# Moving part of a value-page weighting from TensorE to GpSimd and VectorE, with a later attention schedule and an earlier squaring of x

## The reference, cut to what matters

```
h = rms_norm(x, norm1_w);  z = h @ w_in          # conv, q, k, v, memory q and three gates
q, k = partial_rope(rms_norm(...))               # 8 heads, two halves of 64 each
s = einsum('bqhcd,bkhcd->bhcqk', q, k) * 64**-0.5
p = softmax(s);  a = p[:, :, 0] - lam * p[:, :, 1]
o = einsum('bhqk,bkhd->bqhd', a, v)              # prompt: own rows; samples: 16 pages + own row
o = rms_norm(o, subln_w) * 0.8
y_mem = mem_attn(qm, mem_k, mem_v) @ w_cross_out # 4 heads into 256 memory tokens
merged = g0 * y_conv + g1 * (y_diff or y_mem) + ...;  x = x + merged @ w_o
x = x + peer_ffn(rms_norm(x, norm2_w))           # top-16 of 16384 experts, 8 heads, gathered rows
```

## Time and profile before

| | us |
|---|---|
| median of 3 runs | 2854.64 |
| lowest, highest | 2852.84, 2857.38 |
| profiled execution, device time | 2857.79 |
| its span | 2855.9 |
| PE busy in the span | 2478.5 (87%) |
| DVE, POOL, ACT busy | 1390.6 (49%), 1038.9 (36%), 355.1 (12%) |

### The profile page before, as it was taken

The page is one execution under the profiler, slowest core; times in us unless marked ns, Lnnn a source line. Parts: engine busy times, 40 slices in busy tenths (PEclk is TensorE's granted clock), DMA queues, the critical chain, the costliest instruction groups (busy, mean ns, idle before and its releaser), DMA issues.

```text
span 2855.9 us, 28287 instructions
## 1 busy us (share of the span) xinstructions
PE 2478.5 (87%) x9241; PEld 1592.3 (56%) x9241; DVE 1390.6 (49%) x2168; ACT 355.1 (12%) x760; POOL 1038.9 (36%) x952
## 2 busy tenths in 40 slices
PE   6899999979999999999998687777899587777777
PEld 4777788868766668888776333232333133223333
DVE  2365566862112213000057687876555655556543
ACT  2111000012221111000120211101011011111010
POOL 1165566020122210000015556556445443555442
PEclk9999999989999999999999899999899889999999
DMA  5499999594598975443459999999999989999999
GB/s 156 153 335 319 316 337 335 192 332 153 195 339 322 330 275 180 155 138 119 146 200 355 401 421 417 417 417 411 422 422 416 413 360 422 418 421 417 421 422 376
DMA packets 305393, 913.67 MB, mean 320 GB/s; under 512 B 15634, under 2 KB 195946, under 8 KB 236652
## 3 DMA queue, kind: packets, MB, share of 16 engines
q0 software_dynamic: 122304, 723.48, 63.0%
q1 hardware_dynamic: 182980, 188.92, 20.3%
HBM read 905.80 MB, written 6.56 MB: 319 GB/s over the span
## 4 chain that ended last, share of the span: by engine, by line
PE 53%; DMA 25%; DVE 12%; issue 5%; POOL 4%; ACT 1%; DVEq 0%; POOLq 0%; ACTq 0%; SPq 0%
PE ps L573 20%; PE ps L651 12%; DMA sb_S<-in_peer_u_dram,sb_ring 10%; DMA sb_bregion<-in_peer_u_dram,sb_ring 6%; PE ps L663 6%; PE ps L878 4%; DMA sb_mkv<-in_peer_u_dram,sb_ring 3%; PE ps L641 3%; PE ps L751 2%; DVE sb_bregion L1765 2%; DMA sb_wring<-in_w_in_dram 2%; DVE sb_S L1765 2%; DMA sb_S<-in_peer_v_dram,sb_ring 1%; POOL sb_bregion L486 1%; POOL sb_wring L486 1%
## 5 line engine op out<-in xcount | busy, mean ns | idle before, releaser
L878 PE MATMUL ps<-sb_wring,sb_ring 128*128 128x512 f32 x992 | 462.7, 617 | 129.7 <-DMA sb_wring<-in_peer_v_dram,sb_ring 80.8
L573 PE MATMUL ps<-sb_hT,sb_wring 128*128 128x264 f32 x2304 | 533.4, 393 | 18.2 <-DMA sb_wring<-in_w_peer_q_dram 8.7
L573 PEld LDWEIGHTS ps<-sb_hT,sb_wring 128*128 128x128 f32 x2304 | 442.2, 193 | 101.5 <-issue 23.1
L878 PEld LDWEIGHTS ps<-sb_wring,sb_ring 128*128 128x128 f32 x992 | 189.0, 197 | 404.2 <-issue 270.4
L1765 DVE CUSTOM_DVE_ANT_0 sb_bregion<-sb_bregion,sb_rows 128x2048 f32<-128x2048 f32 x128 | 293.6, 2294 | 228.7 <-DMA sb_bregion<-in_peer_u_dram,sb_ring 221.6
L651 PE MATMUL ps<-sb_hT,sb_wring 128*128 128x264 f32 x1536 | 365.8, 389 | 9.2 <-issue 6.8
L651 PEld LDWEIGHTS ps<-sb_hT,sb_wring 128*128 128x128 f32 x1536 | 286.5, 190 | 74.8 <-issue 27.7
L486 POOL DMA_INDIRECT sb_bregion<-in_peer_u_dram,sb_ring x132 | 187.2, 1419 | 280.2 <-DVEq L1183 228.0
L878 PE MATMUL ps<-sb_hT,sb_ring 128*128 128x512 f32 x496 | 234.9, 623 | 46.2 <-DMA sb_hT<-in_peer_v_dram,sb_ring 35.0
L878 PE MATMUL ps<-sb_oreg,sb_ring 128*128 128x512 f32 x496 | 223.4, 597 | 39.8 <-DMA sb_oreg<-in_peer_v_dram,sb_ring 37.2
L1150 ACT ACTIVATE sb_ring<-sb_ident,sb_ring 128x128 f32<-128x128 f32 x248 | 99.6, 402 | 909.5 <-PE ps L878 702.1
(11 more groups left out here) (349 smaller groups left out, 2530.2 us busy)
## 6 DMA issues: line engine op xcount, KB each, us to landing
sb_wring<-in_w_in_dram SPq DMA_DIRECT2D x52, 2048.0 KB, 13.3
sb_ring<-in_cache_k_dram POOLq DMA_DIRECT2D x64, 512.0 KB, 6.5
sb_mkv<-in_cache_k_dram POOLq DMA_DIRECT2D x64, 512.0 KB, 6.8
sb_mkv<-in_cache_v_dram POOLq DMA_DIRECT2D x48, 512.0 KB, 6.9
sb_rows<-in_cache_v_dram POOLq DMA_DIRECT2D x47, 512.0 KB, 7.0
sb_wring<-in_w_mem_kv_dram SPq DMA_DIRECT2D x8, 2048.0 KB, 8.8
sb_wring<-in_w_o_dram SPq DMA_DIRECT2D x8, 2048.0 KB, 8.1
sb_wring<-in_w_peer_q_dram SPq DMA_DIRECT2D x8, 2048.0 KB, 13.7
```

Of the source, the lines that this page charges most:

```text
L573: last = mm(ps[:, (2 * r + c) % 4, 0:NT], wring[:, r, k, c * P:(c + 1) * P], rhs[:, k, :], start=(k == 0), stop=(k == KC - 1))
L878: last = mm(ps[:, 4 * t + q, :], diag[:, k % 4, :], e_slots[v % ER][:, q * 512:(q + 1) * 512], start=False, stop=q_stop, skip_group_check= ...
```

## The change

Three things, in one diff:

1. **Start.** DVE squares x first; the `lam` products come after the copies into `hT`, the column copies after the row factors. The rows of x are no longer multiplied by their factors: DVE multiplies the identity by them (three small tiles), and PE's 16 x 3 transposes become fp32 products with these diagonals.
2. **Units.** Every step of the sample softmax comes later by about a unit, and head `a` runs in units 2a+2 and 2a+3. `turn_maxima(0)` goes from (0, 15) to (1, 23). The branch product of unit 1 goes to bank 5, so that it need not wait for the merge of unit 0.
3. **Value pages.** PE weighs pages 0 to 7 of a sample, in 2 rounds: (odd unit, 18) and (even unit, 10). Pages 8, 9, 11, 13, 14 are multiplied in place by POOL, 10, 12, 15 by DVE, and DVE adds 9 to 15 into page 8, and that into `own_heads` behind `mask_sums`. Page 8 has two slots of its own, the other 15 pages share nine in a ring.

```diff
+        PE_PAGES, BY_POOL, BY_DVE = 8, (8, 9, 11, 13, 14), (10, 12, 15)
+        ORDER = (8, 9, 0, 1, 2, 3, 10, 11, 12, 4, 5, 6, 7, 13, 14, 15)
+            elif n == PE_PAGES:
+                slot = b % 2
+            else:
+                slot, ringed = 2 + ringed % 9, ringed + 1
+        def page_freed(page):
+            if n < PE_PAGES:
+                return "vpage_used", MEM_PAGES + PE_PAGES * b + n + 1
+            if n == PE_PAGES:
+                return "own_summed", b + 1
+            return "page_added", (PAGES - PE_PAGES - 1) * b + n - PE_PAGES
...
+            def weigh_page(b, n):
+                pool.wait_ge(v_landed[slot], 16 * (page_use[b, n] + 1))
+                st(nc.gpsimd.tensor_tensor(page, page, Ad[:, b, n, :].unsqueeze(2).broadcast_to([P, HEADS, DV]), ALU.mult))
+                pool.sem_inc(s["page_weighed"], 1)
-            for p in range(MEM_PAGES, VPAGES):
-                load_page(p)
+            BEHIND = 6
+            for i, (b, n) in enumerate(page_loads):
+                load_page(b, n)
+                if i >= BEHIND and page_loads[i - BEHIND][1] in BY_POOL:
+                    weigh_page(*page_loads[i - BEHIND])
...
-                transpose_rows(x_rows, k, k % 8, TILES).then_inc(s["xT_full"], 1)
+                for t, (first, n) in enumerate(TILES):
+                    last = mm(ps[:, k % 8, first:first + n], x_rows[0:n, t, k * P:(k + 1) * P], small[0:n, t, 0:n], start=True, stop=True)
+                last.then_inc(s["xT_full"], 1)
...
-                pe.wait_ge(s["y_taken"], q + 2)
+                pe.wait_ge(s["y_taken"], q + 2 if bank == 2 else 2)
...
-                pe.wait_ge(s["sums_masked"], m + 1)
+                    pe.wait_ge(s["own_summed"], m - MEM_ROUNDS + 1)
...
-                if (q, k) == (0, 15):
+                if (q, k) == (1, 23):
                     turn_maxima(0, nk)
-                a = (q - 1) // 2
+                a = (q - 2) // 2
-                if 11 <= q < 27 and k in (6, 18):
-                    value_round(MEM_ROUNDS + 2 * (q - 11) + k // 18)
+                if 11 <= q < 27 and (q % 2, k) in ((1, 18), (0, 10)):
+                    value_round(MEM_ROUNDS + q - 11)
...
-            for t in (0, 2):
-                st.run(TSC(x_rows[0:n, t, :], x_rows[0:n, t, :], stat[0:n, t:t + 1], None, ALU.mult))
+            for t, (_, n) in enumerate(TILES):
+                st.run(TSC(small[0:n, t, 0:n], ident[0:n, 0:n], stat[0:n, t:t + 1], None, ALU.mult))
...
+                b = (q - 11) // 2
                 if 13 <= q < 29 and q % 2:
+                    mask_sums(MEM_ROUNDS + b - 1)
+                    add_sums(b - 1)
+                if 11 <= q < 27 and q % 2:
+                    weigh_page(b, 10)
+                    add_page(b, 9)
+                    add_page(b, 10)
+                    weigh_page(b, 12)
+                    add_page(b, 11)
+                    add_page(b, 12)
+                if a < ATTN and q % 2 == 0:
                     maxima_of(a)
+                    if 11 <= q < 27:
+                        add_page(b, 13)
+                        weigh_page(b, 15)
                     normalise(a)
+                    add_page(b, 14)
+                    add_page(b, 15)
```

More of the change, by code:

```diff
@@ L645, in _, with gate_chunk @@
             own_scores()
-            def gate_chunk(b, r, c, q, operand, landed, between=None, ready=None):
+            def gate_chunk(b, r, c, q, operand, landed, between=None, ready=None, bank=2):
                 pe.wait_ge(s["gate_done"], q + 1)
@@ L662, in gate_chunk @@
                 for k in range(BC):
-                    last = mm(ps[:, 2, 0:NT], bwring[:, r, k, c * P:(c + 1) * P], operand[:, k, :], start=(k == 0), stop=(k == BC - 1))
+                    last = mm(ps[:, bank, 0:NT], bwring[:, r, k, c * P:(c + 1) * P], operand[:, k, :], start=(k == 0), stop=(k == BC - 1))
                     if k == BC - 1:
@@ L959, in _ @@
             root(2, stat[:, 3:5])
+            act.wait_ge(s["lam_pre"], 1)
+            st(A_(lam[:, 0:2], lam[:, 0:2], ACT.Exp))
+            act.sem_inc(s["lam_exp"], 1)
             def to_stage(n_chunks, c0, m0):
@@ L1233, in _ @@
                 signal("xT_taken2")
+            dve.wait_ge(s["lam_in"], 64)
+            st(TT(lam4[:, 0, :], lam4[:, 0, :], lam4[:, 1, :], ALU.mult))
+            st(TT(lam4[:, 2, :], lam4[:, 2, :], lam4[:, 3, :], ALU.mult))
+            st(RED(lam[:, 0:1], lam4[:, 0, :], X, ALU.add))
+            st(RED(lam[:, 1:2], lam4[:, 2, :], X, ALU.add))
+            signal("lam_pre")
             row_factors(2, stat[:, 3:5])
@@ L1540, in mask_sums, with weigh_page, add_page, add_sums @@
                 signal("sums_masked")
+            def weigh_page(b, n):
+                slot = page_home[b, n]
+                page = v_slots[slot].rearrange("p (h d) -> p h d", h=HEADS)
+                dve.wait_ge(v_landed[slot], 16 * (page_use[b, n] + 1))
+                st(TT(page, page, Ad[:, b, n, :].unsqueeze(2).broadcast_to([P, HEADS, DV]), ALU.mult))
+            def add_page(b, n):
+                total = v_slots[page_home[b, PE_PAGES]]
+                if n in BY_POOL:
+                    dve.wait_ge(s["page_weighed"], len(BY_POOL) * b + BY_POOL.index(n) + 1)
+                st(TT(total, total, v_slots[page_home[b, n]], ALU.add))
+                signal("page_added")
+            def add_sums(b):
+                st(TT(own_heads, own_heads, v_slots[page_home[b, PE_PAGES]], ALU.add))
+                signal("own_summed")
             of = oflat[:, BC * NT:2 * BC * NT]
@@ L1611, in _ @@
                     maxima_of(a)
+                    if 11 <= q < 27:
+                        add_page(b, 13)
+                        weigh_page(b, 15)
                     normalise(a)
-                if q == 5:
+                if 11 <= q < 27 and q % 2 == 0:
+                    if a >= ATTN:
+                        add_page(b, 13)
+                        weigh_page(b, 15)
+                    add_page(b, 14)
+                    add_page(b, 15)
+                if q == 6:
                     keep_own(q)
```

176 lines of the change are left out of this document (93 added, 83 removed).

## The result

| | before | after |
|---|---|---|
| median, us | 2856.01 | 2972.18 |
| lowest, highest | 2852.84, 2862.03 | 2971.68, 2976.38 |
| runs | 4 | 4 |
| span of the profiled execution | 2855.9 | 2970.0 |

The ratio is 1.0407, 95% interval 1.039 to 1.0424: 116 us slower. The forecast was 2876 with a range of 2845 to 2906, so the direction was right and the size was far too small.

What follows compares the result with a forecast made beforehand. The prediction took PE to bound the value stage, the DMA engines close behind. Start -7, units -15 and value pages +44 (37 plus 7 for port conflicts) made 22 us slower, 2876 against the median 2854.6, range 2845 to 2906.

Steps and rivals of the forecast that it cites:

- 1.35 us a block (all at the low level, 21.6 us): Start: upper bound taken for the 16 blocks of transposing products; the lower bound was 0.85 a block, 13.6 us.
- The rival on the diagonals: Start: the diagonal products don't raise PE's clock; part 1 gives -2 instead of 7, total +31 us; no chance given.
- the old waits, inside the new: Value stage: 1.4 us of existing waits a pair, 8 x 1.4, subtracted in part 3's sum.
- first stall: Before each even unit: PE waits for page 11's multiply, queued behind waiting loads; 7.4 us a sample, eight times.
- r+9.6: Even unit's start: PE restarts 9.6 us after r, the time it leaves a sample's first value round.
- I take 1: Value stage: POOL and DVE multiplies slowing each other, taken as 1 us a sample, 7 us in all.
- The walk: Value stage: step-by-step timing of the queues through one sample, giving 40.3 us a pair of units against 35.4.
- All hidden: Rival, POOL's queue: page 11 weighed before the first round ends, both stalls go; 57 us faster, 2798; chance 0.10.
- Only the first stall: Rival, even unit: DVE runs ahead, so the stall before the columns vanishes; net -5 us, 2850; chance 0.14.
- the second: Before the column sums: PE waits for DVE's list of adds, softmax and merge; 2.8 us, seven times.
- A heavier POOL: Rival, value stage: POOL's multiply with a repeated operand takes twice 2.36 us; net +69, 2923; chance 0.12.
- this ring: Value stage: PE's rounds, POOL's loads and multiplies and DVE's adds wait on each other in turn; 40.3 us against 35.4.

Runs made afterwards that it cites:

- lock_free: Changed kernel with two fills of the same page in place of each GpSimd multiply, five of sixteen pages left unweighed: 2920.35 us (ratio 1.0246).
- pe_busy2: Changed kernel with 15, 8 and 7 unread products on TensorE ahead of its three value-stage waits: 2954.71 us (1.0348).
- free_pages: Changed kernel with every load, wait and signal kept but all multiplies and additions of pages 8 to 15 dropped: 2823.12 us (0.9885).
- behind3: Changed kernel with GpSimd's multiplies 3 loads behind in place of 6: 2900.25 us (1.0159).
- dve_cols: Changed kernel with all eight page multiplies on VectorE, page 14 and the columns reordered in VectorE's list, columns later in TensorE's: 2828.02 us (0.9905).
- behind3_lock_free: Changed kernel with GpSimd's work 3 loads behind in place of 6 and fills in place of its multiplies: 2883.3 us (1.0089).

## Why the prediction failed, step by step

A minus means faster.

**Part 1 (said -7, bounds -8.5 to 2; measured 5.8).** The move of the squares held: PE began at 21.43 where 20.9 was reckoned. The failed step is the ceiling "1.35 us a block (all at the low level, 21.6 us)", which no row gave, and the choice of 15.7 us below it: the products took 26.82 us, 1.68 a block all the way, and 0.95 only when PE had been busy before. Of the 2.9 us hoped for in the first projection 1.4 came. The rival on the diagonals had the right direction and too small a price, 2 us slower for 5.8. I had read the Trainium skill (TensorE: Matmul & The Clock Gate, Part 4: PE-mode transpose), which says that transposes don't make TensorE's clock rise, as a promise that these products would. By their durations they did not in 26.8 us; the granted clock prints 1.00 throughout and settles nothing here.

**Part 2 (said -15; measured -20.6).** The 15 is there at unit 8; the missing 5 is the attention's new place in the pair, which ended the wait behind `keep_columns`. The sum had those 1.4 us a pair too, but took them off part 3, as "the old waits, inside the new".

**Part 3 (said 44; measured 129).** The mechanism was right: first stall said 7.4, found 6.92; restart r+9.6, found r+9.4. Two terms of the sum were mis-sized.

- *"I take 1"* for the port conflicts. They are 6.2 us in the turn shown, since three DVE operations meet a POOL multiply and each lasts 1.9 to 2.3 us longer. Without POOL's multiplies the kernel is 52 us faster, where 7 had been taken. The ceiling was too low as well: with every meeting the price had been put at 3 us a sample, 21 us in all (the 58 for part 3). The Trainium skill (SBUF — State Buffer, SBUF: two separate sides) says that the loser of this port blocks for the whole of the winner's instruction, and the 1.9 to 2.3 us beside a multiply of 1.91 agree. It limits this to a GpSimd operation that reads SBUF, and lock_free's fills, which read nothing, agree with that too.
- *PE at full speed behind its stalls.* The walk used durations from a stage whose clock was 1.00. Its stalls of 6.92 and 3.62 us are followed by stretches at 0.50 (from 898 and from 930), and in a ring, late PE is late for the next link. The rows of the turn hold 5.2 us of it; pe_busy2's pairs are 4.1 us shorter.

With the two, 6.2 and 5.2 us, and the 1.0 of gaps, less 0.9 for two POOL multiplies of 1.91 where 2.36 was reckoned, the walk's 40.3 becomes 51.8, against 51.9 measured in this turn. Why other pairs are up to 2.4 us longer is not taken apart. A third stall, 3.69 us before the weights are turned back, was not in the walk at all: it goes with the 2.25 and 2.05 us that page 15's multiply and the softmax's last step are held up, and lock_free doesn't have it.

**The rivals.** *All hidden* was put at 2798 and was not to be had: free_pages gives 2823. But its mechanism (weigh page 11 before the loads that wait) is what behind3 does, for 72 us. *Only the first stall*: the second is there, 3.62 us for the 2.8 of the walk. *A heavier POOL*: POOL's multiply with a repeated operand is lighter than the plain one, 1.91 for 2.36.

## What to carry to other kernels

Before work moves to an idle engine, read what the bound engine would gain at most (here 16 us, with the transfers at 0.90 already), then write out the queues: a constant of the loads' lead was worth 72 us, and the place of three entries, two in VectorE's list and one in TensorE's, 57. GpSimd's multiplies beside whole-tile operations on VectorE were no parallel work here: price each meeting at the full length of GpSimd's. And price a stall of TensorE at more than its length: behind the stalls of this ring it ran slow, which cost 4 to 5 us a turn.

## What was not expected of the hardware

- DVE's operation lasts 1.9 to 2.3 us longer when a POOL multiply of 1.91 lies over it, and POOL's mostly does not get longer; in the earlier trace rows both did. By the printed starts DVE was first in the three meetings of the turn above, by 0.09 to 0.47 us, and was held even so. Where it was 0.58 us ahead (below, changed kernel) it kept its 1.22 and POOL's multiply took 2.40. So who comes first can't be read from starts that are half a microsecond apart. POOL's fills of the same tiles, 1.76 us a page, hold nobody.

```profile
1019.25 1.22 DVE L1586 TENSOR_TENSOR sb_rows<-sb_rows,sb_Ad 128x1024 f32<-128x1024 f32 x1
1019.83 2.40 POOL L468 TENSOR_TENSOR sb_mkv<-sb_mkv,sb_Ad 128x1024 f32<-128x1024 f32 x1
```

- 96 fp32 records of 128 columns with a weight load each: 26.8 us from rest, 15.25 behind 14 us of products, with a printed clock of 1.00 both times. Where the clock's column says nothing, durations must.
- The length of an idle alone doesn't tell what TensorE does behind it. In dve_cols an idle of 2.65 us left the next record of a value round at 0.59 us and one of 2.52 was followed by 1.01, as those of 3.04 and 3.75 were by slow ones. behind3_lock_free's columns behind 3.17 us took 1.92, and behind 3.16 us 3.54. Rows of dve_cols:

```profile
826.37 0.59 PE L795 MATMUL ps<-sb_rows,sb_Ad 128*8 128x512 f32 x1 [2.65 <-DMA sb_S<-in_cache_v_dram]
961.38 3.55 PE L795 MATMUL ps<-sb_rows,sb_Ad 128*8 128x512 f32 x16 [3.04 <-DMA sb_rows<-in_cache_v_dram]
996.05 1.01 PE L795 MATMUL ps<-sb_S,sb_Ad 128*8 128x512 f32 x1 [2.52 <-DMA sb_rows<-in_cache_v_dram]
```
